# Forget-gate attention pairs: k's hi and lo parts by thirds, and the last v product in eight steps among maxima and key blocks

## The chip, the core and the metric

One core of a Trainium2 chip runs the whole program. The metric is the device time of one execution, in microseconds (us). Engines in the rows: PE is TensorE (PEld its weight loads), DVE is VectorE, ACT is ScalarE, POOL is GpSimd, SP is SyncE, which issues the DMAs. Each engine works through its own queue in order; semaphores tie them together.

## The reference

One step of a hybrid encoder layer over 1024 prompt rows and 32 sample rows of width 1024: a SwiGLU block, a mixer, a second SwiGLU block, all in float32. The change lies in one of the mixer's three head groups, the forgetting attention (8 heads of 64, here in 4 pairs of heads):

```python
q, k, v, f_logit = ...                      # columns of rms(x) @ w_in
q = rms_per_head(q) * gq;  k = rms_per_head(k) * gk
logf = log_sigmoid(f_logit + b_f)
k_all, v_all = concat(past_k, k), concat(past_v, v)
cum = cumsum(concat(past_logf, logf))
s = q @ k_all.T * 64 ** -0.5 + cum_q[:, None] - cum_k[None, :]
s = where(kpos <= qpos, s, -inf)
y = softmax(s) @ v_all                      # k, v and logf are outputs too
```

The matrix products keep float32 precision: each operand is split into a hi part (rounded to fp32r) and a lo part (the rest), and a product is hi*hi + hi*lo + lo*hi.

## The kernel before

`MIXER` runs two conv groups, four "fox" groups (one pair of forget-gate heads each, `attend(g)` for g = 0 to 3, called first to fourth pair here) and two memory groups. The pairs begin at about 919, 1014, 1101 and 1188 us; the memory groups follow at 1274. Engines run separate programs, and `attend(g)` exists once for each.

**Projections.** `PROJ["fox"]` lists nine products, n = 0 to 8: q, k and v, each in three chunks of rows (384, 384, 288 columns of the moving operand, `CHUNKS`). `product` works through the 8 blocks of the model width (KT), three matmuls to a block (L252 to L254), into the bank `PBANK[n]`. For q and k, ScalarE squares the result (L1201), TensorE sums the squares over a head (`head_sums`, L1999), ScalarE makes a rough 1/root with Ln and Exp (`head_rough`, L875 and L877, banks 6 and 7 in turn), VectorE refines it and scales (`normed`: L1294, L1296, L1298, L1658) into `qT` or `kT`. For v, ScalarE copies to `vT` (L1196). `bank_free` lets a product into a used bank only when its reader is done: product 6 (the first of v) takes bank 0, which held q's first chunk and then the turned cached keys (`turn_past`, copied by `past_keys`, L1124).

**Parts of k.** ScalarE writes q's hi parts (`q_hi(c)`, L1138 and the like, after products 2, 3 and 4) and, after product 7, both hi parts of k over all 1184 keys (`k_hi`, L1130). VectorE copies the other halves (`k_twice`, L1666) and makes the lo parts (`k_lo`, L1673), after all three k chunks.

**Tokens.** `TT` lists the turns of k and v to token-major layout (`turn_tokens`, L2037; ScalarE copies them out in `tokens`, L1147 for k, L1150 for v): three for k, three for v. SyncE stores them (`store_tokens`). In the first pair TensorE also turns the forget sums (L2152) once `tokens(0)` is copied, and only then SyncE loads the minus-F rows (L637).

**Maxima.** `scores(n)`, L2062, for 18 units (2 of samples, 8 row tiles for each head) in banks 6-7 and 4-5 by turns; VectorE takes each row's maximum (`smax`, L1694). `scores(1)` waits until the k tokens are out of banks 4 and 5; from n = 2, `scores(n)` waits for `smax(n-2)`, from n = 10 for `smax(n-1)`. `turn_max` and `turn_four` (L2076, L2077) turn the maxima to rows, ScalarE copies them (`maxima`, L1164). Units 10 to 17 lie in the next stretch.

**Key blocks.** For each of 28 blocks: `keyed(n)` (scores with keys on the partitions, L2104, L2105, mask L2107), `exps(n)` on ScalarE (L1175), and two blocks later `weigh(n-2)` (L2120). `keyed(0)` waits for the first two rows of maxima.

GpSimd splits the next group's weights (`split_in`, L804 and L787) when this group's products and k parts are done.

Of the kernel before, what the change touches and what calls it, by code (L numbers as in the profile page):

```python
# [31 lines left out]
def hybrid_step(nc, i, o):  # L32
# [30 lines left out]
    with ctx:  # L63
# [198 lines left out]
        PBANK = {"fox": [0, 1, 2, 3, 4, 5, 0, 1, 2], "mem": [0, 1, 2, 3, 4]}  # L262
# [16 lines left out]
        def nrm_count(kind, m):  # L279
# [4 lines left out]
        TT = {"fox": [("k", 0, 4, 3), ("k", 4, 4, 4), ("k", 8, 1, 5), ("v", 0, 4, 0), ("v", 4, 4, 1), ("v", 8, 1, 3)],  # L284
              "mem": [("k", 0, 2, 3), ("v", 0, 2, 4)]}
# [21 lines left out]
        KEND = {"fox": KEYS, "mem": 2 * NMEM}  # L307
# [42 lines left out]
        NB = {k: len(BLOCKS[k]) for k in BLOCKS}  # L350
        NSTORED = {"fox": 96, "mem": 48}
# [89 lines left out]
        def _(sp):  # L441
# [198 lines left out]
            def store_tokens(g):  # L640
# [4 lines left out]
                last = NTT["fox"] // 2 if kind == "fox" else 1  # L645
# [92 lines left out]
        def _(pool):  # L738
# [56 lines left out]
            def split_in(v):  # L795

                if MIXER[v - 1][0] == "conv":
                    pool.wait_ge(CONVS["proj"], 9 * v)
                else:
                    pool.wait_ge(A["proj"], upto(NPROJ, v - ITER["conv"]))  # L800
                    pool.wait_ge(A["kdve"], 4 * (v - ITER["conv"]))
# [52 lines left out]
        def _(act):  # L854
# [255 lines left out]
            def attend(g):  # L1110
# [9 lines left out]
                def past_keys():  # L1120
                    act.wait_ge(A["cturned"], g + 1)
                    act.wait_ge(A["kdve"], 4 * g)
# [3 lines left out]
                def k_hi():  # L1126
                    act.wait_ge(A["past"], g + 1)
                    act.wait_ge(A["nrm"], nrm0 + NRM[kind])
                    for j in range(PAIR):
                        act.activation(KS1[half_rows(j), j, 0:KEND[kind]], kT[half_rows(j), 0:KEND[kind]], ACT.Copy)\  # L1130
                            .then_inc(A["khi"], 1)
# [9 lines left out]
                def tokens(q):  # L1141
                    what, t0, nt, b = TT[kind][q]
                    act.wait_ge(A["tturned"], tt0 + q + 1)
                    n = tile_rows(kind, t0)
                    src = bank(b, nt * P, n).rearrange("p (t n) -> p t n", t=nt)
# [43 lines left out]

                if g == 0:  # L1190
                    act.wait_ge(s_init, 7)
                for n, (what, _, c) in enumerate(PROJ[kind]):
                    s, w = span(kind, n)
                    act.wait_ge(A["proj"], proj0 + n + 1)
                    if what == "v":
                        act.activation(vT[:, s:s + w], bank(PBANK[kind][n], w), ACT.Copy).then_inc(A["vcopied"], 1)  # L1196
                    else:
                        m = NORMED[kind].index(n)
# [14 lines left out]
                    if n in (2, 3, 4):  # L1213
                        q_hi(n - 2)
                    if kind == "fox" and n == 7:
                        k_hi()
                        act.wait_ge(A["stored"], upto(NSTORED, g))
                        tokens(0)
                    if kind == "fox" and n == 8:
                        tokens(1)  # L1220
                        tokens(2)
                if kind == "mem":
                    k_hi()
# [3 lines left out]
                else:  # L1227
                    tokens(3)
                    tokens(4)
                    tokens(5)  # L1230
# [52 lines left out]
        def _(dve):  # L1283
# [357 lines left out]
            def attend(g):  # L1641
# [19 lines left out]
                def k_twice():  # L1661

                    dve.wait_ge(A["past"], g + 1)
                    dve.wait_ge(A["nrm"], nrm0 + NRM[kind])
                    for j in range(PAIR):
                        dve.tensor_copy(KS1[half_rows(1 - j), j, 0:KEND[kind]], kT[half_rows(j), 0:KEND[kind]])\  # L1666
                           .then_inc(A["kdve"], 1)

                def k_lo():
                    for j in range(PAIR):  # L1670
                        dve.wait_ge(A["khi"], 2 * g + j + 1)
                        r = half_rows(j)
                        dve.tensor_tensor(KS2[r, j, 0:KEND[kind]], kT[r, 0:KEND[kind]],  # L1673
                                          KS1[r, j, 0:KEND[kind]].bitcast(F32), ALU.subtract).then_inc(A["kdve"], 1)

# [41 lines left out]
                for m in range(NSQ[kind]):  # L1717
# [68 lines left out]
        def _(pe):  # L1786
# [28 lines left out]
            def product(b, block, x_hi, x_lo, s, w, fresh=None):  # L1815


                for k in range(KT):
# [166 lines left out]
            def attend(g):  # L1985
# [36 lines left out]
                def turn_tokens(q):  # L2022
                    what, t0, nt, b = TT[kind][q]
# [231 lines left out]
```

## Time and profile before

| | |
|---|---|
| median of 3 runs | 2303.93 us (2303.18 to 2308.80) |
| profiled execution, its time | 2305.36 us |
| profiled execution, its span | 2303.2 us |
| mean granted TensorE clock | 0.955 |
| busy in the span | PE 92%, PEld 87%, DVE 52%, ACT 36%, POOL 15% |
| first to last instruction of TensorE's second pair | 1014.5 to 1100.7 us |

A row of a timeline reads: start, duration, engine, line, operation, output<-inputs, shapes, how many instructions were merged (x2), and in brackets how long the engine stood before it and who ended that wait. A duration of x2 is from the first's start to the last's end. A granted clock of 1.00 is 2.4 GHz, 0.50 is 1.2 GHz.

### The profile page before, as it was taken

The numbers are of one execution on the slowest core, as the hardware profiler recorded it, in microseconds if no ns is written. First come the engines' busy times: TensorE is split into PE (matmuls) and PEld (weight loads), VectorE is DVE, ScalarE is ACT, GpSimd is POOL, SyncE is SP. The second block draws the span as 40 slices with busy tenths as digits, with TensorE's granted clock in tenths as the row PEclk, the third lists the DMA queues.
The fourth block names the chain that finished last, engine by engine and source line by source line (L and its number), as shares of the span: only waits on it lengthen the run. The fifth ranks groups of instructions, "written<-read, shape, count | busy, mean of one in ns | idle before, by whom it ended". The sixth has DMA issues, their size and how long they took to land.

```text
span 2303.2 us, 37130 instructions
## 1 busy us (share of the span) xinstructions
PE 2115.3 (92%) x15188; PEld 1994.7 (87%) x15188; DVE 1206.0 (52%) x2097; ACT 824.8 (36%) x1375; POOL 346.7 (15%) x175
## 2 busy tenths in 40 slices
PE   4889999999999879799999779968899999999996
PEld 3789999999999879676876657958899999999996
DVE  6795665586330072545545555179755666843103
ACT  5342223244231240455555454054322223533213
POOL 0000000003444423101101203000000000143440
PEclk7899999999999989899999889979999999999997
DMA  4542222247543216321220125024322223485222
GB/s 150 140 121 75 84 84 70 78 131 290 176 130 92 93 57 47 90 61 42 57 61 22 47 84 184 1 94 147 91 76 77 84 84 99 152 297 168 89 68 85
DMA packets 239736, 234.76 MB, mean 102 GB/s; under 512 B 28297, under 2 KB 181513, under 8 KB 239057
## 3 DMA queue, kind: packets, MB, share of 16 engines
q1 hardware_dynamic: 239568, 232.39, 33.6%
q8 instruction: 122, 2.00, 0.4%
q14 instruction: 46, 0.37, 0.1%
HBM read 182.56 MB, written 49.80 MB: 101 GB/s over the span
## 4 chain that ended last, share of the span: by engine, by line
PE 81%; DVE 10%; issue 3%; ACT 3%; DMA 2%; SPq 1%; POOL 0%; DVEq 0%; ACTq 0%
PE banks L252 23%; PE banks L253 23%; PE banks L254 23%; PE banks L2120 4%; PE banks L2062 1%; PE banks L2104 1%; PE banks L1833 1%; PE banks L2105 1%; DVE scores_minusF L1694 1%; DVE hforms_lo L1459 1%; DVE w_lo L1353 1%; DMA x_again<-x_spill 1%; DMA out_conv_state_sample<-conv_in 1%; PE banks L1999 1%; DVE hforms_f L1443 1%
## 5 line engine op out<-in xcount | busy, mean ns | idle before, releaser
L252 PE MATMUL banks<-hforms_hi,w_hi 128*128 128x264 f32 x2112 | 607.2, 288 | 57.0 <-issue 34.0
L253 PE MATMUL banks<-hforms_lo,w_hi 128*128 128x264 f32 x2112 | 607.7, 288 | 0.0
L254 PE MATMUL banks<-hforms_hi,w_lo 128*128 128x264 f32 x2112 | 606.1, 287 | 0.0
L252 PEld LDWEIGHTS banks<-hforms_hi,w_hi 128*128 128x128 f32 x2112 | 404.6, 192 | 61.9 <-issue 47.7
L780 POOL TENSOR_TENSOR w_lo<-w_raw,w_hi 128x1024 fp32r<-128x1024 f32 x88 | 219.3, 2496 | 1382.3 <-ACT w_hi L985 1382.3
L254 PEld LDWEIGHTS banks<-hforms_hi,w_lo 128*128 128x128 f32 x2112 | 403.6, 191 | 0.0
L253 PEld LDWEIGHTS banks<-hforms_lo,w_hi 128*128 128x128 f32 x2112 | 403.2, 191 | 0.0
L254 PE MATMUL banks<-acts_a,w_lo 128*128 128x264 f32 x896 | 256.5, 286 | 0.0
L252 PE MATMUL banks<-acts_a,w_hi 128*128 128x264 f32 x896 | 254.4, 284 | 1.7 <-DVE acts_a L1477 1.7
L253 PE MATMUL banks<-acts_a,w_hi 128*128 128x264 f32 x896 | 255.2, 285 | 0.0
L252 PE MATMUL banks<-h_hi,w_hi 128*128 128x384 f32 (+1 forms) x576 | 198.0, 344 | 23.0 <-DVE h_lo L1311 10.2
L985 ACT ACTIVATE w_hi<-w_raw 128x1024 fp32r<-128x1024 f32 x88 | 93.2, 1059 | 348.3 <-PE banks L254 307.0
L253 PE MATMUL banks<-h_lo,w_hi 128*128 128x384 f32 (+1 forms) x576 | 189.1, 328 | 0.0
L254 PE MATMUL banks<-h_hi,w_lo 128*128 128x384 f32 (+1 forms) x576 | 188.1, 327 | 0.0
L1493 DVE SCALAR_TENSOR_TENSOR xT<-banks,xT 128x264 f32<-128x264 f32 x64 | 23.9, 432 | 298.0 <-PE banks L254 298.0
L252 PEld LDWEIGHTS banks<-acts_a,w_hi 128*128 128x128 f32 x896 | 170.1, 190 | 2.2 <-issue 2.0
L254 PEld LDWEIGHTS banks<-acts_a,w_lo 128*128 128x128 f32 x896 | 168.4, 188 | 0.0
L253 PEld LDWEIGHTS banks<-acts_a,w_hi 128*128 128x128 f32 x896 | 168.3, 188 | 0.0
L918 ACT ACTIVATE w_hi<-w_sums 128x1024 fp32r<-128x1024 f32 x90 | 95.6, 1062 | 190.1 <-DVE w_sums L1341 116.1
L254 PE MATMUL banks<-acts_b,w_lo 128*128 128x264 f32 x512 | 146.6, 286 | 0.0
L253 PE MATMUL banks<-acts_b,w_hi 128*128 128x264 f32 x512 | 145.8, 285 | 0.0
L252 PE MATMUL banks<-acts_b,w_hi 128*128 128x264 f32 x512 | 145.2, 284 | 0.0
(257 smaller groups left out, 4101.9 us busy)
## 6 DMA issues: line engine op xcount, KB each, us to landing
w_raw<-in_w_ffn_down SPq DMA_DIRECT2D x88, 512.0 KB, 4.2
w_raw<-in_w_ffn_gate SPq DMA_DIRECT2D x60, 512.0 KB, 5.2
w_raw<-in_w_ffn_up SPq DMA_DIRECT2D x60, 512.0 KB, 5.2
act_rows<-act_f SPq DMA_DIRECT2D x44, 528.0 KB, 2.8
acts_f<-act_rows SPq DMA_DIRECT2D x44, 528.0 KB, 5.2
xT<-x_spill SPq DMA_DIRECT2D x3, 4224.0 KB, 16.6
w_raw<-in_w_in SPq DMA_DIRECT2D x20, 512.0 KB, 6.0
x_spill<-xT SPq DMA_DIRECT2D x4, 2112.0 KB, 9.3
```

Source lines behind the costliest of these rows:

```text
L252: eng.matmul(out, w_hi, x_hi, start=first, stop=False, skip_group_check=added)
L253: eng.matmul(out, w_hi, x_lo, start=False, stop=False, skip_group_check=added)
L254: return eng.matmul(out, w_lo, x_hi, start=False, stop=last, skip_group_check=added)
L780: pool.tensor_tensor(wlo[:, e % 4, :], raw[:, e % 4, :], whi[:, e % 4, :].bitcast(F32), ALU.subtract)\
L918: act.activation(slots(whi, wxh, G[q], n), src, ACT.Copy).then_inc(f[f"{which}_hi"], 1)
L985: act.activation(whi[:, e % 4, :], raw[:, e % 4, :], ACT.Copy).then_inc(f["wd_hi"], 1)
L1353: dve.tensor_tensor(slots(wlo, wxl, slot, 1), r[:, at:at + 1, :], slots(whi, wxh, slot, 1).bitcast(F32), ALU.subtract).then_inc(f[f"{which ...
L1443: dve.scalar_tensor_tensor(q[:, first:last + 1:last - first, :], x.rearrange("p (h n) -> p h n", h=2), gain[:, 2 * n, k:k + 1], nr[:, s:s ...
L1459: dve.tensor_tensor(HL[z][:, :, kk, :], FT[:, m % 2, 0:7, :], HH[z][:, :, kk, :].bitcast(F32), ALU.subtract).then_inc(f["forms_lo"], 1)
L1493: dve.scalar_tensor_tensor(xT[:, d, s:s + QC], bank(DBANK[e], QC), 0.5, xT[:, d, s:s + QC], ALU.mult, ALU.add).then_inc(f["resid"], 1)
L1694: dve.tensor_tensor_reduce(junk[0:rows, 0:w], PS[0:rows, b:b + w], nF[0:rows, j, k0:k0 + w], 1.0, -3e38, ALU.add, ALU.max, m).then_inc(A[" ...
L2120: pe.matmul(PS[:, 512 * ob + oc:512 * ob + oc + w], VO[0:kr, vo, j, :], PRT[0:kr, (b0 + n) % 4, 0:w], start=first, stop=last, skip_group_c ...
```

## The change

- k's parts are made in thirds (`KPARTS`), each as soon as its chunk is scaled. ScalarE does `k_hi(0)`, `k_hi(1)`, `k_hi(2)` at the end of steps n = 4, 5, 6 of its projection loop, VectorE `k_parts(c)` right behind `normed(3 + c)`. The last third (with the cached keys, 416 columns) also waits for `past_keys`. q's last third moves from n = 4 to n = 3 on ScalarE, and its lo part from m = 3 to m = 2 on VectorE.
- Product 8 (the last of v) leaves the projections. TensorE does its blocks 0 to 2 between `scores(9)` and `turn_four(0, 1)`, behind a wait for `smax(8)` (it now uses bank 7), blocks 3 and 4 behind `turn_four(0, 1)`, and blocks 5, 6 and 7 in the key-block steps 0, 1 and 2.
- The v tokens become four turns: tiles 0 to 3, 4 and 5 in the maxima as before, tiles 6 and 7 and tile 8 (bank 7) at step 5 of the key blocks. ScalarE's v copy of product 8 stands behind `exps(2)`, its copies of the two turns behind `exps(5)`.
- Waits follow: `scores(0)` for all hi parts and copies, GpSimd for all nine products, `weigh` of v tiles 6 to 8 for the last copy, SyncE's v stores likewise. The memory groups compute as before.

```diff
-        PBANK = {"fox": [0, 1, 2, 3, 4, 5, 0, 1, 2], "mem": [0, 1, 2, 3, 4]}
+        PBANK = {"fox": [0, 1, 2, 3, 4, 5, 0, 1, 7], "mem": [0, 1, 2, 3, 4]}
+        V_EARLY, V_TURNED = 3, 5
+        V_BEHIND = {-1: (3, 4), 0: (5,), 1: (6,), 2: (7,)}
+        KPARTS = {"fox": [(0, 384), (384, 384), (768, KEYS - 768)], "mem": [(0, 2 * NMEM)]}
...
 # ScalarE
-                def k_hi():
-                    act.wait_ge(A["past"], g + 1)
-                    act.wait_ge(A["nrm"], nrm0 + NRM[kind])
+                def k_hi(c):
+                    s, w = KPARTS[kind][c]
+                    if c == NKP[kind] - 1:
+                        act.wait_ge(A["past"], g + 1)
+                    act.wait_ge(A["nrm"], nrm0 + nrm_count(kind, 3 + c))
...
-                    if n in (2, 3, 4):
-                        q_hi(n - 2)
+                    for c in {"fox": {2: (0,), 3: (1, 2)}, "mem": {2: (0,), 3: (1,), 4: (2,)}}[kind].get(n, ()):
+                        q_hi(c)
+                    if kind == "fox" and n in (4, 5, 6):
+                        k_hi(n - 4)
...
                     exps(n)
+                    if kind == "fox" and n == max(V_BEHIND):
+                        v_copy(8)
+                    if kind == "fox" and n == V_TURNED:
+                        tokens(5)
+                        tokens(6)
...
 # VectorE
-                    if m == 3:
+                    if m == (2 if kind == "fox" else 3):
                         q_lo(2)
-                k_twice()
-                k_lo()
+                    if m >= 3:
+                        k_parts(m - 3)
...
 # TensorE
+                def last_v(steps):
+
+                    s, w = span(kind, 8)
+                    for k in steps:
+                        if k == 0:
+                            pe.wait_ge(A["smax"], 18 * g + 9)
+                        mm = product(PBANK[kind][8], 2, hh, hl, s, w, None, (k,))
+                        if k == KT - 1:
+                            mm.then_inc(A["proj"], 1)
...
                 scores(9)
+                if kind == "fox":
+                    last_v(range(V_EARLY))
                 turn_four(0, 1)
+                if kind == "fox":
+                    last_v(V_BEHIND[-1])
                 for n in range(NB[kind] + 2):
                     if n < NB[kind]:
                         keyed(n)
                     if n >= 2:
                         weigh(n - 2)
+                    if kind == "fox":
+                        last_v(V_BEHIND.get(n, ()))
+                        if n == V_TURNED:
+                            turn_tokens(5)
+                            turn_tokens(6)
```

## Rows read from the trace of the kernel before

**Rows 1.** The page, chain that ended last, shares of the span by engine.
```profile
PE 81%; DVE 10%; issue 3%; ACT 3%; DMA 2%; SPq 1%; POOL 0%; DVEq 0%; ACTq 0%
```

**Rows 2.** Timeline of ScalarE, third pair, 1118 to 1141 us.
```profile
1122.85 0.49 ACT L1201 ACTIVATE head_squares<-banks 128x384 f32<-128x384 f32 x1 [1.12 <-PE banks L254]
...
1124.70 0.90 ACT L1138 ACTIVATE q_hi_lo<-qT 64x288 fp32r<-64x288 f32 x2
...
1126.78 0.41 ACT L1201 ACTIVATE head_squares<-banks 128x288 f32<-128x288 f32 x1 [0.25 <-PE banks L254]
...
1131.59 0.49 ACT L1196 ACTIVATE vT<-banks 128x384 f32<-128x384 f32 x1 [3.02 <-PE banks L254]
...
1136.65 2.40 ACT L1130 ACTIVATE k_hi_twice<-kT 64x1184 fp32r<-64x1184 f32 x2
...
1139.07 0.60 ACT L1147 ACTIVATE k_by_token<-banks 128x512 f32<-128x512 f32 x1
...
1140.32 0.74 ACT L1147 ACTIVATE k_by_token<-banks 128x512 f32<-128x512 f32 x2
```

**Rows 3.** Timeline of VectorE, third pair, refinement of k's thirds to maximum 0.
```profile
1124.67 0.56 DVE L1294 SCALAR_TENSOR_TENSOR head_rstd<-banks,head_r 128x384 f32<-128x384 f32 x1 [1.79 <-ACT head_r L877]
...
1126.45 0.62 DVE L1658 SCALAR_TENSOR_TENSOR kT<-banks,head_gains,head_rstd 128x384 f32<-128x384 f32 x1
...
1133.09 0.46 DVE L1294 SCALAR_TENSOR_TENSOR head_rstd<-banks,head_r 128x288 f32<-128x288 f32 x1 [2.08 <-ACT head_r L877]
...
1134.57 0.64 DVE L1658 SCALAR_TENSOR_TENSOR kT<-banks,head_gains,head_rstd 128x256 f32<-128x256 f32 x2
...
1137.86 2.80 DVE L1673 TENSOR_TENSOR k_lo_and_one<-kT,k_hi_twice 64x1184 fp32r<-64x1184 f32 x2 [0.98 <-ACT k_hi_twice L1130]
...
1140.71 0.31 DVE L1694 CUSTOM_DVE_ANT_0 scores_minusF<-banks,minusF 32x160 f32<-32x160 f32 x1
```

**Rows 4.** Timeline of TensorE, third pair: first k tokens, scores 1, `keyed(0)`.
```profile
1136.07 0.60 PE L2037 MATMUL banks<-ident,kT 128*128 128x128 f32 x4
...
1141.11 0.26 PE L2062 MATMUL banks<-k_hi_twice,q_hi_lo 128*32 128x160 f32 x1 [0.54 <-ACT k_by_token L1147]
...
1150.45 0.80 PE L2104 MATMUL banks<-q_hi_lo,k_hi_twice 128*128 128x512 f32 x1 [0.68 <-ACT q_hi_and_max L1164]
```

**Rows 5.** Windows: length, PE, PEld, DVE, ACT, POOL busy, clock, DMA share, GB/s.
```profile
960.00:985.00 25.00, 18.60 (x90) 12.17 (x88) 9.26 (x33) 6.40 (x17) 10.08 (x6) 0.73 0.58 157
...
1053.00:1073.00 20.00, 16.57 (x86) 10.82 (x85) 10.77 (x31) 7.62 (x20) 10.07 (x6) 0.91 0.22 55
...
1139.00:1159.00 20.00, 16.79 (x82) 10.69 (x80) 10.40 (x30) 7.67 (x20) 10.09 (x6) 0.83 0.22 54
...
1158.00:1178.00 20.00, 18.98 (x92) 11.77 (x91) 8.95 (x16) 11.40 (x21) 0.00 (x0) 1.00 0.20 65
...
1149.00:1150.00 1.00, 0.33 (x1) 0.13 (x1) 0.40 (x2) 0.19 (x1) 1.00 (x1) 0.93 0.00 0
...
1150.00:1151.00 1.00, 0.55 (x1) 0.50 (x2) 0.00 (x0) 0.40 (x1) 1.00 (x1) 0.50 0.02 8
```

**Rows 6.** Timeline of TensorE, third pair, last matmuls of two blocks of product 8.
```profile
1139.15 0.30 PE L254 MATMUL banks<-h_hi,w_lo 128*128 128x288 f32 x1
...
1139.55 0.30 PE L254 MATMUL banks<-h_hi,w_lo 128*128 128x288 f32 x1
```

**Rows 7.** Timelines of ScalarE, TensorE, SyncE, VectorE and TensorE, first pair.
```profile
945.31 0.91 ACT L1138 ACTIVATE q_hi_lo<-qT 64x288 fp32r<-64x288 f32 x2 [0.75 <-DVE qT L1658]
...
946.34 0.81 PE L1999 MATMUL banks<-head_squares,ones_over_head 128*128 128x384 f32 x2
...
960.83 0.82 SPq L637 DMA_DIRECT2D minusF<-negF_rows  x2
...
966.82 0.31 DVE L1694 CUSTOM_DVE_ANT_0 scores_minusF<-banks,minusF 32x160 f32<-32x160 f32 x1 [4.88 <-DMA minusF<-negF_rows]
...
978.29 0.50 PE L2104 MATMUL banks<-q_hi_lo,k_hi_twice 128*128 128x512 f32 x1 [0.68 <-ACT q_hi_and_max L1164]
```

More of the change, by code:

```diff
@@ L350, in hybrid_step @@
         NB = {k: len(BLOCKS[k]) for k in BLOCKS}
+        NKP = {k: len(KPARTS[k]) for k in KPARTS}
         NSTORED = {"fox": 96, "mem": 48}
@@ L644, in store_tokens @@
                 c = it * P
-                last = NTT["fox"] // 2 if kind == "fox" else 1
+                last = 3 if kind == "fox" else 1
                 sp.wait_ge(A["tcopied"], upto(NTT, g) + last)
@@ L1141, in tokens @@
                 def tokens(q):
-                    what, t0, nt, b = TT[kind][q]
-                    act.wait_ge(A["tturned"], tt0 + q + 1)
+                    what, t0, nt, b, at = TT[kind][q]
+                    act.wait_ge(A["tturned"], tt0 + max(x for x, y in enumerate(TT[kind]) if y[0] == what and y[3] == b) + 1)
                     n = tile_rows(kind, t0)
-                    src = bank(b, nt * P, n).rearrange("p (t n) -> p t n", t=nt)
+                    src = PS[0:n, 512 * b + at:512 * b + at + nt * P].rearrange("p (t n) -> p t n", t=nt)
                     if what == "k":
@@ L1188, in sum_rough, with v_copy @@
                     act.activation(lr[r, 0:w], lr[r, 0:w], ACT.Exp, scale=-1.0).then_inc(A["rough_sum"], 1)
+                def v_copy(n):
+                    s, w = span(kind, n)
+                    act.wait_ge(A["proj"], proj0 + n + 1)
+                    act.activation(vT[:, s:s + w], bank(PBANK[kind][n], w), ACT.Copy).then_inc(A["vcopied"], 1)
                 if g == 0:
@@ L1193, in attend @@
                     s, w = span(kind, n)
-                    act.wait_ge(A["proj"], proj0 + n + 1)
+                    if kind == "fox" and n == 8:
+                        break
                     if what == "v":
-                        act.activation(vT[:, s:s + w], bank(PBANK[kind][n], w), ACT.Copy).then_inc(A["vcopied"], 1)
+                        v_copy(n)
                     else:
+                        act.wait_ge(A["proj"], proj0 + n + 1)
                         m = NORMED[kind].index(n)
@@ L1227, in attend @@
                 else:
-                    tokens(3)
-                    tokens(4)
-                    tokens(5)
+                    for q in range(1, 5):
+                        tokens(q)
                 for x in range(3):
@@ L1813, in norm_mean, with product @@
                 pe.matmul(bank(MBANK + c, w), onesD[:, :], nsum[:, 0:w], start=True, stop=True).then_inc(NORM[n]["mean"], 1)
-            def product(b, block, x_hi, x_lo, s, w, fresh=None):
-                for k in range(KT):
+            def product(b, block, x_hi, x_lo, s, w, fresh=None, steps=range(KT)):
+                for k in steps:
                     if fresh:
@@ L2022, in turn_tokens @@
                 def turn_tokens(q):
-                    what, t0, nt, b = TT[kind][q]
+                    what, t0, nt, b, at = TT[kind][q]
                     if kind == "mem":
@@ L2083, in turn_four @@
                             pe.wait_ge(A["mcopied"], 5 * g + 4)
+                        else:
+                            pe.wait_ge(A["tcopied"], tt0 + NTT[kind])
                     elif h:
-                        pe.wait_ge(A["tcopied"], tt0 + NTT[kind])
+                        pe.wait_ge(A["tcopied"], tt0 + 1)
+                        if g == 0:
+                            pe.wait_ge(fg["copied"], 5)
                     else:
@@ L2108, in keyed, with e_of @@
                     mm.then_inc(A["keyed"], 1)
+                def e_of(vo):
+                    return 6 <= vo <= PT
+                def last_v(steps):
+                    s, w = span(kind, 8)
+                    for k in steps:
+                        if k == 0:
[3 more added lines that the diff above has]
+                            mm.then_inc(A["proj"], 1)
                 def weigh(n):
@@ L2114, in weigh @@
                     if n == 0:
-                        pe.wait_ge(A["tcopied"], tt0 + NTT[kind])
+                        pe.wait_ge(A["tcopied"], tt0 + (5 if kind == "fox" else 2))
+                    elif kind == "fox" and e_of(vo):
+                        pe.wait_ge(A["tcopied"], tt0 + 7)
                     if q0 == SEQ and first:
@@ L2124, in attend @@
                     s, w = span(kind, n)
+                    if kind == "fox" and n == 8:
+                        break
                     pe.wait_ge(W["lo"], 3 * v + b + 1)
```

56 lines of the change are left out of this document (24 added, 32 removed).

## The prediction

> **What bounds the kernel now.** I read the page first: TensorE carries four fifths of the chain that ended last [rows 1]. The change touches only the four forget-gate pairs, which run between 919 and 1274 us. There I read the timeline of each engine for the third pair (the second and fourth repeat it to about 0.4 us), looking for places where TensorE stands, and then the windows for the clock.
>
> A pair has three stretches. In the projections TensorE is never kept waiting from the second pair on. ScalarE and VectorE run behind it: square, sum on TensorE, rough root on ScalarE (L875, L877), VectorE's refinement and scaling (L1294 to L1658) [rows 2, 3]. Then come the maxima. Scores 0 starts when the last product is done, scores 1 when ScalarE has copied k's turned tokens [rows 2, 4]. From there VectorE sets the pace, until the second group of four maxima is turned and copied; TensorE idles before `keyed(0)` at 1150.45 [rows 4]. Last come the key blocks, where TensorE is full, 18.98 of 20 us [rows 5].
>
> The clock matters as well. In the microsecond from 1149 TensorE is busy for 0.33 us, and at its end the granted clock goes from 1.0 to 0.5, that is from 2.4 to 1.2 GHz [rows 5]. From the mean clocks, half speed lasts 2*(1-0.91)*20 = 3.6 us in the second pair, 2*(1-0.83)*20 = 6.8 us in the third and 2*(1-0.73)*25 = 13.5 us in the first, whose gap while the minus-F rows are loaded is long [rows 5, 7].
>
> **The maxima do not start when the last product leaves.** The last v product, 288 columns, is eight blocks with 0.40 us from one to the next [rows 6], 3.2 us. Taking it out of the projections would start the maxima 3.2 us earlier if k's parts were ready. They aren't, because of ScalarE's new order. `k_hi(c)` stands in ScalarE's queue ahead of the next square or v copy, which stand ahead of the next rough root, and VectorE's next refinement needs that root. What was two engines overlapping becomes one chain. Per third:
> - VectorE's refinement, 1124.67 to 1126.45+0.62: 2.40; for the last, narrower third 1133.09 to 1134.57+0.64: 2.12 [rows 3].
> - `k_hi(c)`: two instructions. 288 columns take 0.90/2 = 0.45, 1184 take 2.40/2 = 1.20 [rows 2]; in between, 384 columns are about 0.53 and 416 about 0.56. A third is 1.07, the last 1.12.
> - square or v copy, then rough root: v copy at 1131.59 to refinement at 1133.09, 1.50 [rows 2, 3].
>
> The third thirds of q come ahead of the k parts too: a pair of q instructions of 0.9, twice, 1.8 us, go into an idle gap of 1.12 [rows 2], and delay the next square by 0.7 and the root behind it by 0.5. Sum for the third pair: 1124.67+0.5 = 1125.2; +2.40 +1.07 +1.50 = 1130.1; +2.40 +1.07 +1.50 = 1135.1; +2.12 = 1137.2. Before it was 1134.57+0.64 = 1135.2, so k is finished 2.0 us **later**. Then ScalarE: 1.12 for its last part, 0.4 for the v copy that waits behind it, 0.60+0.74 for the k tokens: 1140.1. It was 1140.32+0.74 = 1141.06 [rows 2]. Scores 1, which started at 1141.11, gains **1.0 us**, not 3.2. VectorE's own share (it copies the other halves while ScalarE works, and two differences of a third take 2.8*416/1184, about 1.0, against 2.80) ends near 1139.3, and the whole-width copy and difference no longer hold scores 0; they aren't last [rows 3]. TensorE stands from 1136.1 (first k tokens, [rows 4]) to 1137.2, turns nine tiles in about a microsecond and stands again to 1140.1.
>
> **The maxima and their gap.** Three of the nine v turns leave (four take 0.60, so about 0.1 each in a row); they end a short wait of VectorE: 0.1 to 0.2 more. The first three blocks start when maximum 8 is done and take 1.2 us, in TensorE's idle time, but the turns of maxima 6 to 8 now queue behind them: up to 0.1 lost. Blocks 3 and 4, 0.8 us, lie beside ScalarE's copy of the row of maxima (idle 0.68 [rows 4]); 0.1 sticks out. `keyed(0)`: 1.1 us earlier.
>
> **The key blocks.** Three blocks, 1.2 us, stand on full TensorE, and three turns, 0.3 to 0.45. Each change from scores or values to a product costs a first matmul that starts its successor late: none to 0.15 each way here, estimated, since no row shows these neighbours. Sum 1.5 to 2.2; I take **1.9**, near the top, since TensorE has no slack there. ScalarE's v copy and token copies are added behind exps 2 and 5; they wait for TensorE, and exps 3 and 6 wait behind them. Values are consumed two blocks later, so I cost this at nothing; without that lag it would be the copies, 0.4 and about 1. GpSimd's split of the next weights now waits for the last block, some 13 us later; it takes 10.09 us, GpSimd is idle for the next 20 [rows 5], and the next pair starts at 1188: nothing. SyncE's v stores wait for tokens 6, some 13 us later, ahead of the minus-F load, which waits for the last maximum anyway: nothing.
>
> Per pair without the clock: -1.1+1.9 = +0.8.
>
> **The clock.** Five blocks in the gap before `keyed(0)` keep TensorE busy there, and the late fall should go. While TensorE is full, half speed costs half its length: (3.6+6.8+3.6)/2 = 7.0 in the second to fourth pair (the fourth falls like the second), less 0.5 for what TensorE stands in it [rows 5]. Gain 6.5. But a **new gap** opens, 1136.1 to 1140.1, four microseconds with about one of work. The old fall came in a gap with a third of work [rows 5], so I expect a fall here in two or three of the four. It hits the maxima, where VectorE sets the pace: in the first pair, at half speed, maximum 0 to `keyed(0)` was 978.29-966.82 = 11.5 us, in the third 1150.45-1140.71 = 9.7 [rows 3, 4, 7]. Price 1.5 each, to 1.8.
>
> The Trainium skill, "TensorE: Matmul & The Clock Gate", section "HAM oscillation — how this bites in real kernels", says that a product whose work between two waits is short is throttled in every round and starts cold each time. By that rule the time would be -0.8+4.5, 2307.6, since all three pairs would pay; the trace agrees so far that every pair has its fall.
>
> **The first pair** is worse off. ScalarE waits for q's last third, which VectorE's forget sums delay: it starts at 945.31 [rows 7] and takes 1.8. Square 0.5, root 1.1 and past keys 0.25 behind it end at 948.95. The head sum of k's first third waits for that square instead of running at 946.34, and the first v product, about 0.4 behind it (half of 0.81 for two), waits for the past keys' bank [rows 7]: TensorE stands 2.2 us. The chain gives 948.7 +2*(2.40+1.07+1.50) +2.12 = 960.8 for k. The turn of the F rows waits for the first k tokens' copy (1.12+0.4+0.6 later, 962.9), the load of minus F is issued 0.8 behind, 963.7 instead of 960.83, and maximum 0 hangs on that load (a wait of 4.88 [rows 7]). **+2.9**, +1.9 in the key blocks, -1.5 if a second fall near 979 goes: +3.3.
>
> **Sum.** 3*0.8 - 6.5 + 3.3 = -0.8; with new falls in two to three pairs, 3 to 4.5 more: +2 to +4. I take +2.1. The profiled execution's span of 2303.2 becomes 2305.3, its time 2305.4 becomes 2307.5; the median lay 1.4 lower, 2303.93, and becomes **2306.0**.
>
> **Rivals.**
> - *The order of ScalarE does not bind* (the change's obvious promise). Maxima start 3.1 us earlier in every pair, the first one's load 2.8: 4*(1.9)-3*3.1-2.8-6.5-1.5 = -12.5, 2291.4. For it: TensorE alone. Against: k's root stands behind `k_hi` in one queue, and ScalarE is in order.
> - *The new gap does not lower the clock.* Nine turns may be work enough: -0.8 and some stalls less than reckoned, 2300 to 2303.
> - *Slower: half speed outlasts the maxima.* In the first pair it lasted through the whole of the maxima. If the fall in the new gap still holds at `keyed(0)`, the old 6.5 is not gained and the early five blocks take twice as long, +1.0 a pair: 3*(0.8+1.5+1.0), and 2.9+1.9+1.0 in the first, = +15.7 less what a part of the pairs escapes; 10 to 16, 2314 to 2320. It decides when half speed lasts over 10 us from 1138.
>
> **How the numbers follow.** Forecast with two or three new falls 0.50 (2302 to 2311), clock kept 0.24, half speed through the gap 0.15, order not binding 0.11. A measurement tells about 0.3% from none, 6.9 us. Of the forecast nearly all is within that; a tenth of the rival with the clock kept is beyond it, and most of the third. Faster 0.12, same 0.74, slower 0.14. Stages behind the pairs run unchanged, but their own clock falls may shift by a microsecond or two. Range for 8 in 10: 2297 to 2314, which leaves out the ends of both far rivals; the likeliest case's own is 2302 to 2311.
>
> **What would show it.** Right: ScalarE's k parts each directly followed by a square or v copy that was ready long before; the last refinement of k near 2 us later in the pair; TensorE with one microsecond of work in four before scores 1; the last product's blocks 0 to 4 at full clock in the old gap; in the first pair 2 us of standing ahead of the first v product, minus F issued 3 us later. Wrong: maxima 3 us earlier, or key blocks no longer than before (then the steps fell into waits I don't see), or clock falls at places that follow no gap.

## The result, and the profile after

The changed kernel took 2314.27 us in the median of five runs (2309.83 to 2315.76), the kernel before 2305.01 in the median of five beside it (2303.18 to 2308.80): ratio 1.0037, interval 1.0022 to 1.0052. Later, on another chip, it was 2311.35 (12 runs) against 2306.27 (26 runs): 1.0023, interval 1.0012 to 1.0035. So the change costs between 0.1 and 0.5%, about what was taken for the limit of what can be told. The forecast was 2306.0 within 2297 to 2314. The first median lies 0.3 us above that range, the second within it. One execution of the late `k_hi` below (8570.1 us) and one of the move only (2352.76) were in a slow state, and no ratio here uses them.

The profiled execution took 2309.83, its span was 2307.7 against 2303.2. The page, the second row as in [rows 1]:

```profile
PE 2121.9 (92%) x15188; PEld 1999.7 (87%) x15188; DVE 1211.2 (52%) x2129; ACT 828.8 (36%) x1399; POOL 347.0 (15%) x175
...
PE 80%; DVE 9%; ACT 4%; issue 3%; DMA 2%; SPq 1%; POOL 0%; DVEq 0%; ACTq 0%
```

These shares say nothing on the change. It is seen pair by pair. Lengths in us, each worked out from the first product of a pair to that of the next (the first pair from the turn of the past keys on); "memory" are the two groups behind the pairs, which run the same steps in both kernels:

| | 1st | 2nd | 3rd | 4th | pairs | memory |
|---|---|---|---|---|---|---|
| before | 71.46 | 86.21 | 87.26 | 85.93 | 330.9 | 130.9 |
| changed | 74.75 | 87.82 | 87.23 | 86.81 | 336.6 | 135.1 |

The pairs lost 5.7 us, the memory groups 4.2; the stretch ahead of the pairs was 4.6 shorter, the one behind the memory groups 0.9 shorter: +4.5 with rounding, the difference of the spans. The repeats below tell which of these belong to the change.

The second pair of the changed kernel, which answers to [rows 2] and [rows 3]. First ScalarE, then VectorE. For comparison with the third pair of before, subtract 1035.76 here and 1123.30 there, the turns of the past keys.

```profile
1034.22 0.91 ACT L1147 ACTIVATE q_hi_lo<-qT 64x288 fp32r<-64x288 f32 x2
1036.10 0.49 ACT L1217 ACTIVATE head_squares<-banks 128x384 f32<-128x384 f32 x1
...
1040.21 1.07 ACT L1139 ACTIVATE k_hi_twice<-kT 64x384 fp32r<-64x384 f32 x2 [2.30 <-DVE kT L1676]
1041.31 0.41 ACT L1217 ACTIVATE head_squares<-banks 128x288 f32<-128x288 f32 x1
...
1045.35 1.08 ACT L1139 ACTIVATE k_hi_twice<-kT 64x384 fp32r<-64x384 f32 x2 [2.46 <-DVE kT L1676]
1046.45 0.49 ACT L1202 ACTIVATE vT<-banks 128x384 f32<-128x384 f32 x1
...
1050.20 1.12 ACT L1139 ACTIVATE k_hi_twice<-kT 64x416 fp32r<-64x416 f32 x2 [2.25 <-DVE kT L1676]
...
1051.74 1.21 ACT L1156 ACTIVATE k_by_token<-banks 128x512 f32<-128x512 f32 x3
```

```profile
1037.79 0.56 DVE L1312 SCALAR_TENSOR_TENSOR head_rstd<-banks,head_r 128x384 f32<-128x384 f32 x1 [1.47 <-ACT head_r L884]
...
1042.92 0.56 DVE L1312 SCALAR_TENSOR_TENSOR head_rstd<-banks,head_r 128x384 f32<-128x384 f32 x1 [0.80 <-ACT head_r L884]
...
1047.98 0.46 DVE L1312 SCALAR_TENSOR_TENSOR head_rstd<-banks,head_r 128x288 f32<-128x288 f32 x1 [0.72 <-ACT head_r L884]
...
1049.46 0.64 DVE L1676 SCALAR_TENSOR_TENSOR kT<-banks,head_gains,head_rstd 128x256 f32<-128x256 f32 x2
```

Each engine waits for the other in turn: ScalarE's `k_hi(c)` for VectorE's scaled third, VectorE's next refinement for ScalarE's root, with a square or v copy right behind each `k_hi` that had long been ready. The refinements stand 5.13 and 5.06 apart. VectorE stands 0.80 and 0.72 us before the second and the third of them, for ScalarE's root: its own parts of k, which now lie between the refinements too, don't hold them.

TensorE in the same pair, answering to [rows 4]:

```profile
1050.16 1.20 PE L2052 MATMUL banks<-ident,kT 128*128 128x128 f32 x9 [1.48 <-DVE kT L1676]
1051.58 0.23 PE L2076 MATMUL banks<-k_hi_twice,q_hi_lo 128*32 128x160 f32 x1 [0.21 <-ACT k_hi_twice L1139]
...
1053.00 0.34 PE L2076 MATMUL banks<-k_hi_twice,q_hi_lo 128*32 128x160 f32 x1 [1.07 <-ACT k_by_token L1156]
...
1064.91 0.50 PE L2122 MATMUL banks<-q_hi_lo,k_hi_twice 128*128 128x512 f32 x1
```

It waits 1.48 for k, turns nine tiles, and waits twice more. The windows (length, busy time of PE, PEld, DVE, ACT, POOL, clock, DMA share, GB/s) are the new gap and the maxima of the second pair, twenty microseconds of the second, third and fourth, and the second pair's key blocks:

```profile
1050.00:1053.00 3.00, 1.55 (x11) 1.12 (x12) 2.34 (x7) 2.70 (x6) 0.00 (x0) 0.90 0.00 0
...
1053.00:1063.00 10.00, 9.88 (x39) 7.05 (x40) 6.02 (x17) 2.07 (x7) 0.00 (x0) 0.52 0.19 55
...
1050.00:1070.00 20.00, 18.43 (x92) 13.76 (x93) 10.09 (x31) 7.70 (x19) 0.92 (x1) 0.74 0.10 28
...
1138.00:1158.00 20.00, 18.10 (x96) 13.41 (x96) 9.98 (x30) 8.20 (x19) 1.61 (x2) 0.83 0.10 28
...
1228.00:1248.00 20.00, 19.70 (x100) 14.13 (x101) 9.27 (x28) 6.61 (x15) 4.72 (x4) 0.83 0.10 28
...
1068.00:1088.00 20.00, 18.97 (x91) 11.63 (x90) 7.46 (x15) 11.17 (x24) 10.12 (x6) 1.00 0.32 91
```

After the gap the maxima run at 0.52, half speed. By the means it lasts 2*(1-0.74)*20 = 10.4 us in the second pair and 6.8 in the third and fourth. TensorE looks busier there than before (9.88 of 10) and yet does the maxima more slowly. The fall is in the maxima of all three pairs, and the late one of [rows 5] is gone.

### The profile page after: what moved, and what is told of

Its sections match the earlier page's. It is cut to its first block, busy times and chain, and to the rows that moved or that the text cites. A ratio compares the mean times of both kernels' runs of the same rounds, so it can differ in the third digit from the quotient of the medians.

```text
span 2307.7 us, 37198 instructions
## 1 busy us (share of the span) xinstructions
PE 2121.9 (92%) x15188; PEld 1999.7 (87%) x15188; DVE 1211.2 (52%) x2129; ACT 828.8 (36%) x1399; POOL 347.0 (15%) x175
## 4 chain that ended last, share of the span: by engine, by line
PE 80%; DVE 9%; ACT 4%; issue 3%; DMA 2%; SPq 1%; POOL 0%; DVEq 0%; ACTq 0%
PE banks L252 23%; PE banks L253 23%; PE banks L254 22%; PE banks L2154 4%; PE banks L2076 2%; PE banks L1851 1%; PE banks L2122 1%; PE banks L2123 1%; DMA x_again<-x_spill 1%; DVE hforms_lo L1477 1%; DMA out_conv_state_sample<-conv_in 1%; DVE w_lo L1371 1%; DVE scores_minusF L1712 0%; DVE head_rstd L1316 0%; DVE head_rstd L1314 0%
```

## The experiments

Between what the maxima wait for (k's order), the clock in the new gap, and the product's blocks in the key blocks, the times alone can't decide, since they overlap. So each part was done alone, undone alone, or covered. Times in the following table are us from the turn of the past keys, second, third and fourth pair (one figure where all agree):

| | scores 1 | maximum 0 | `keyed(0)` |
|---|---|---|---|
| before | 17.81 | 17.41 | 27.54, 27.15, 27.15 |
| changed | 17.24 | 16.48 | 29.15, 28.56, 28.15 |
| thirds only | 19.50 | 19.10 | 28.83, 28.84, 29.18 |
| move only | 17.04 | 17.40 | 28.42, 28.77, 28.36 |
| late `k_hi` | 15.12 | 15.95 | 25.27, 26.82, 26.64 |
| gap filled | 17.24 | 16.48 | 26.75, 26.74, 27.11 |
| product in the maxima | 15.12 | 15.96 | 25.08, 25.28, 25.43 |
| q's last third back | 16.79 | 16.04 | 28.04, 27.70, 26.65 |

**The changed kernel again.** No edit.

> The changed kernel once more, unchanged, beside the others. Theory A (ScalarE's queue makes one chain of k's thirds, the new gap of four microseconds lowers the clock, and what is left of the difference is clock falls in the memory groups that differ from execution to execution): the four pairs are again longer by 3.3, 1.6, 0.0 and 0.9 us within 1 us each, since their instructions repeat; the memory groups and the stretch ahead of the pairs may differ by 2 to 5 us from the first profile; median +5 to +10. Theory B (the memory groups are slower by the change itself): they are again 4 us longer than in the kernel before.

2311.35 us, ratio 1.0023. The profiled execution was its longest, span 2315.4: pairs 75.10, 87.22, 86.78, 86.66, together 335.8; memory groups 136.7. The pairs repeat, with a fall in each again. In the fourth it was short this time, 2*(1-0.91)*20 = 3.6 us:

```profile
1228.00:1248.00 20.00, 17.55 (x100) 12.88 (x100) 10.41 (x31) 8.24 (x20) 2.30 (x2) 0.91 0.10 28
```

**Thirds only**: k's parts by thirds in the kernel before, with q's last third one step earlier as in the change; the last product stays where it was.

```diff
-                    if n in (2, 3, 4):
-                        q_hi(n - 2)
+                    for c in {"fox": {2: (0,), 3: (1, 2)}, ...}[kind].get(n, ()):
+                        q_hi(c)
-                        k_hi()
+                    if kind == "fox" and n in (4, 5, 6):
+                        k_hi(n - 4)
...
-                k_twice()
-                k_lo()
+                    if m >= 3:
+                        k_parts(m - 3)
```

> The kernel before with k's parts by thirds alone, product 8 where it was. Theory A: k is finished 2.0 us later, TensorE stands 1.4 us before the first k tokens with product 8 still behind them, scores 1 starts 1.4 us later, the late clock fall before keyed(0) stays: +1.4 a pair, +4 to +5 in the first, +9 in all. Rival (the thirds are free or a gain, and the moved product costs): within 1 us of before in each pair, or faster, since the last difference on VectorE is a third as long.

2316.63 us (6 runs), ratio 1.0045, 1.0029 to 1.0061. TensorE, second pair (the turn of the past keys at 1041.25), and the window of its maxima and key blocks:

```profile
1055.63 0.66 PE L2041 MATMUL banks<-ident,kT 128*128 128x128 f32 x4 [1.45 <-DVE kT L1662]
...
1060.73 0.26 PE L2066 MATMUL banks<-k_hi_twice,q_hi_lo 128*32 128x160 f32 x1 [0.54 <-ACT k_by_token L1150]
...
1060.00:1104.00 44.00, 39.90 (x199) 24.56 (x197) 18.64 (x49) 23.43 (x52) 9.61 (x6) 1.00 0.19 55
```

The first k tokens come 14.38 after the turn, against 12.77 before (1136.07-1123.30): the new order costs 1.6 us ahead of the tokens in each pair, 1.7 at scores 1. About 0.44 of it is q's last third (the run with that third back, below), the other 1.2 k's thirds. The last product then fills what was the new gap, and the clock stays up: second pair 86.13, no longer than before. The fourth is 86.47, the third 87.70 with a fall behind `keyed(0)`. The expectation had the late fall in every pair; it is missing in the second and the fourth, and why isn't settled. The first pair is hit hardest: 78.47, +7.0. The four together take 338.8, 7.7 more than before. This is the part of the change that costs.

**The move only**: the changed kernel with k's parts whole again, and they and q's last third where they were.

```diff
-        KPARTS = {"fox": [(0, 384), (384, 384), (768, KEYS - 768)], ...}
+        KPARTS = {"fox": [(0, KEYS)], ...}
...
                     if kind == "fox" and n == 7:
+                        k_hi(0)
...
+                k_parts(0)
```

> The changed kernel with k whole again (hi parts, copies and lo parts after the last third, q's last third where it was), so the moved product alone. Theory A: the gap on TensorE is there too, since k's whole parts and tokens take ScalarE until 4 us after product 7; scores 1 gains 0.6 us, VectorE's whole difference holds maximum 0, key blocks +1.9, clock falls in the new gap instead of the old one: +0.6 a pair, first pair 0, +2 in all. Rival (the moved product is the loss): +1.5 a pair or more, like the changed kernel.

2309.42 us (12 runs), ratio 1.0018, 1.0005 to 1.0031. Second pair, VectorE's difference and what TensorE waits for; then its window:

```profile
1050.14 2.81 DVE L1690 TENSOR_TENSOR k_lo_and_one<-kT,k_hi_twice 64x1184 fp32r<-64x1184 f32 x2 [0.97 <-ACT k_hi_twice L1139]
...
1051.58 0.24 PE L2074 MATMUL banks<-k_hi_twice,q_hi_lo 128*32 128x160 f32 x1 [2.08 <-DVE k_lo_and_one L1690]
...
1052.62 0.26 PE L2074 MATMUL banks<-k_hi_twice,q_hi_lo 128*32 128x160 f32 x1 [0.70 <-ACT k_by_token L1156]
...
1048.00:1068.00 20.00, 16.66 (x91) 12.63 (x90) 11.41 (x28) 8.37 (x17) 0.00 (x0) 0.83 0.10 28
```

Scores 1 is 0.77 earlier than before, but maximum 0 stays at 17.40: VectorE starts it behind its 2.81 of whole-width difference. The gap is there and with it the fall; `keyed(0)` comes 0.9 to 1.6 us later than before. The first pair takes 71.20, as before. The four together take 332.8, +1.8. Thirds or move, each alone is slower than before; together, at 2311.35, they lie between the two.

**`k_hi` one place later, q's last third back**: the changed kernel, with ScalarE's k thirds behind the square or v copy and root that VectorE needs next, VectorE's parts one step later as well, and q's last third as in the kernel before (by the same lines as under "Q's last third back" below).

```diff
-                    if kind == "fox" and n in (4, 5, 6):
-                        k_hi(n - 4)
+                    if kind == "fox" and n in (5, 6):
+                        k_hi(n - 5)
+                    if kind == "fox" and n == 6:
+                        k_hi(2)
...
-                    if m >= 3:
-                        k_parts(m - 3)
+                    if kind == "fox" and m >= 4:
+                        k_parts(m - 4)
+                if kind == "fox":
+                    k_parts(2)
```

> The changed kernel with ScalarE's k_hi(0) and k_hi(1) one step later, behind the next rough root, k_hi(2) behind k_hi(1), q's last third where it was, and VectorE's parts one step later likewise. Theory A: ScalarE no longer waits for VectorE ahead of a root, k is finished when it was in the kernel before, scores 1 starts 2.8 us earlier than before, TensorE's gap before it is about 2 us and no clock fall follows: -3 a pair, -2.5 in the first, -12 us in all, faster than both. Rival (ScalarE's order does not matter, the moved product costs): like the changed kernel, +5 to +9.

2298.76 us, ratio 0.9966, 0.9955 to 0.9977: faster than before. ScalarE and TensorE in the second pair (turn at 1032.67), then the windows of the second and third:

```profile
1044.70 1.12 ACT L1139 ACTIVATE k_hi_twice<-kT 64x416 fp32r<-64x416 f32 x2 [1.28 <-DVE kT L1678]
...
1045.44 1.14 PE L2058 MATMUL banks<-ident,kT 128*128 128x128 f32 x9
...
1047.50 0.24 PE L2082 MATMUL banks<-k_hi_twice,q_hi_lo 128*32 128x160 f32 x1 [0.92 <-DVE k_hi_twice L1688]
1047.78 0.27 PE L2082 MATMUL banks<-k_hi_twice,q_hi_lo 128*32 128x160 f32 x1
```

```profile
1045.00:1065.00 20.00, 17.54 (x105) 12.68 (x104) 12.14 (x35) 8.37 (x20) 2.82 (x2) 1.00 0.10 28
...
1129.00:1149.00 20.00, 18.64 (x98) 13.31 (x96) 11.48 (x33) 7.81 (x19) 1.31 (x2) 0.83 0.10 28
```

The k tokens come at 12.77 again, without a wait (1045.44-1032.67), and scores 1 at 15.12, 2.7 us earlier than before. That is nearly the gain that the first rival promised, and what withheld it was the order of the queues. This run moves both ScalarE's and VectorE's; that ScalarE's was the one that bound is read from the waits of the changed kernel above. Maximum 0 gains less, 1.5 us (15.95 against 17.41): VectorE starts it behind its own parts of k. The pairs are 69.52, 83.96, 85.49, 85.33, together 324.3 against 330.9. The expectation had -12 us with no clock fall; it was -7.5. The third and fourth still fall to half speed, the second doesn't, though the three have the same instructions at the same times up to maximum 0. Why the second escapes is not settled.

**The gap filled**: the changed kernel with 17 matmuls of 288 columns in the gap of each pair, nine ahead of the k tokens and eight between scores 0 and scores 1. Their result is used by nobody; all else is computed as before.

```diff
                     if kind == "fox" and n == 7:
+                        filler(9)
                         turn_tokens(0)
...
                 scores(0)
+                if kind == "fox":
+                    filler(8)
                 scores(1)
```

> The changed kernel with 17 matmuls of 288 columns added in the new gap of each pair, whose result nobody reads: 9 (1.2 us) ahead of the first k tokens, 8 (1.0 us) between scores 0 and scores 1. Both are places where TensorE stands 1.5 and 1.1 us. Theory A (the new gap lowers the clock, and half speed over the maxima costs 2.3 to 3.3 us): no fall behind the gap in pairs two to four, maximum 0 to keyed(0) about 9.5 us instead of 11.5 to 12.7, each pair 2 to 3 us shorter, 6 to 8 in all. Rival (more matmuls are more work, or the fall comes from the maxima themselves): pairs as long as before this edit or longer by 0.5.

2309.30 us (10 runs) against 2309.97 on the same chip (17 runs): 1.0008, 0.9995 to 1.0020. TensorE's k tokens, second pair, and the windows that answer to those of the changed kernel:

```profile
1054.13 1.20 PE L2052 MATMUL banks<-ident,kT 128*128 128x128 f32 x9 [0.28 <-DVE kT L1676]
...
1053.00:1073.00 20.00, 18.42 (x115) 13.70 (x113) 11.46 (x34) 8.22 (x20) 2.25 (x2) 1.00 0.10 28
...
1139.00:1159.00 20.00, 18.27 (x112) 13.39 (x111) 11.19 (x34) 8.62 (x20) 2.82 (x2) 1.00 0.10 28
...
1224.00:1244.00 20.00, 18.06 (x113) 13.35 (x112) 11.11 (x34) 8.14 (x19) 2.04 (x2) 1.00 0.10 28
```

In these three pairs scores 1 and maximum 0 start where they did in the changed kernel, so up to there nothing else moved; the clock stays at 1.0 and `keyed(0)` comes 2.4, 1.8 and 1.0 earlier. The fourth is 0.4 later than its twins (27.11) without any fall, after VectorE stood once for 0.49 us in the maxima. The first pair keeps its long gap at the load of minus F and its fall. The pairs are 85.44, 85.42, 85.79, the first 74.54: together 331.2, where the three executions of the changed kernel have 336.6, 335.8 and 335.5. That the idle gap lowers the clock, and what this costs, is shown by this run.

**The product in the gap and in the maxima**: the order of the late `k_hi`, product 8 in steps of its blocks where TensorE stood (two ahead of the scores, one at maximum 6, one at 8, four behind the ninth scores), none left in the key blocks; maximum 0 writes to bank 0, so that bank 2 is free for the product.

```diff
-        V_BEHIND = {-1: (3, 4), 0: (5,), 1: (6,), 2: (7,)}
+        V_AT = {0: (0, 1), 6: (2,), 8: (3,), 9: (4, 5, 6, 7)}
...
-        PBANK = {"fox": [0, 1, 2, 3, 4, 5, 0, 1, 7], ...}
+        PBANK = {"fox": [0, 1, 2, 3, 4, 5, 0, 1, 2], ...}
```

> The kernel with the late k_hi (e3_late_k_hi), and product 8 in bank 2: blocks 0 and 1 ahead of scores 0, 2 behind scores 6, 3 behind scores 8, 4 to 7 behind scores 9, its v copy ahead of the copy of the second four maxima, the turns of v tiles 6 to 8 right behind that turn; the first maxima are turned into bank 0. No block lies in the key blocks any more. Theory A: the key-block stretch falls from 36.1 to 34.8 us, keyed(0) moves by no more than 0.3, the clock falls in fewer pairs: pairs of 82.5 to 83.5, 5 to 8 us less than e3_late_k_hi, 13 to 15 less than the kernel before. Rival (the blocks are on the path wherever they stand): pairs as in e3_late_k_hi, 84 to 85.5.

2293.0 us (6 runs), ratio 0.9940, 0.9922 to 0.9957: it beats both kernels. Windows over the maxima and the key blocks of the second pair, and over the maxima of the third and fourth:

```profile
1046.00:1066.00 20.00, 19.20 (x112) 13.24 (x110) 12.39 (x36) 8.63 (x23) 8.76 (x6) 1.00 0.10 28
...
1058.00:1078.00 20.00, 18.88 (x90) 11.31 (x90) 8.20 (x19) 10.62 (x23) 9.14 (x6) 1.00 0.32 92
...
1130.00:1150.00 20.00, 19.09 (x105) 12.48 (x104) 11.88 (x35) 7.84 (x22) 10.13 (x6) 1.00 0.11 31
1212.00:1232.00 20.00, 18.84 (x107) 12.67 (x107) 11.77 (x35) 7.82 (x22) 9.50 (x6) 1.00 0.10 28
```

No fall in these pairs. They take 67.97, 82.36, 82.56, 82.71, together 315.6, 15.3 less than before. From `keyed(0)` to the next pair it is 34.72 us, where the changed kernel has 36.11 at full clock too: three blocks and three turns in the key blocks cost 1.39. The thirds only agree: 34.73 in the two pairs without a fall. GpSimd's split of the next weights lies in the key blocks here too (9.14 of 20 us) and costs nothing there, as forecast. The expectation of 82.5 to 83.5 a pair held but for 0.1.

**Q's last third back**: the changed kernel with `q_hi(2)` one step later on ScalarE and `q_lo(2)` one later on VectorE.

```diff
-                    for c in {"fox": {2: (0,), 3: (1, 2)}, ...}[kind].get(n, ()):
-                        q_hi(c)
+                    if n in (2, 3, 4):
+                        q_hi(n - 2)
...
-                    if m == (2 if kind == "fox" else 3):
+                    if m == 3:
                         q_lo(2)
```

> The changed kernel with q's last third alone where it was (ScalarE step 4, VectorE behind m = 3). Theory A: in the first pair TensorE no longer stands before k's head sum; it still waits for the past keys' bank only if ScalarE is late, so 1.5 to 2.2 us come back there; in the others k is finished up to 0.5 us earlier, the pairs change by less than 0.7. Rival: the first pair's loss is the chain of k's thirds and the load of minus F alone, no change there.

2307.93 us, one run. Scores 1 comes 0.44 earlier than in the changed kernel (16.79 against 17.23), which prices the move of q's last third in the later pairs. In the first pair the head sum of k's first third (L2017) runs without the wait that it has in the changed kernel, shown in the section below:

```profile
945.50 0.81 PE L2017 MATMUL banks<-head_squares,ones_over_head 128*128 128x384 f32 x2
```

The first pair is 72.46 against 74.75: 2.3 of the 3.3 that it lost come from q's last third, not from k's.

The other three take 86.72, 86.36 and 85.34. The second and third are 0.4 to 0.5 shorter than where the changed kernel has a fall of the same length (87.22, 86.78). The fourth is 1.3 shorter, more than the 0.7 expected, since its clock does not fall:

```profile
1137.00:1157.00 20.00, 17.70 (x94) 13.12 (x94) 10.78 (x33) 7.89 (x19) 1.10 (x2) 0.83 0.10 28
1224.00:1244.00 20.00, 16.87 (x101) 12.18 (x102) 10.88 (x34) 8.61 (x20) 2.79 (x2) 1.00 0.10 28
```

The four together are 330.9, what the kernel before takes. So in this one execution the whole loss of the change is gone once q's last third stands where it was; about 1 us of that is the fall that the fourth pair was spared.

**The kernels again**, no edit: before, before, changed.

> The kernel before, unchanged, for a second profile. Theory A: the four pairs repeat to within 1 us (71.5, 86.2, 87.3, 85.9), with one late clock fall each; the memory groups, 130.9 us in the first profile, may be 133 to 137 here, as in every profile of the changed kernels, because their clock falls differ by execution. Theory B (the change slows the memory groups): 131 again.

> The kernel before a third time, to settle the memory groups, whose two profiles so far gave 130.9 and 131.1 us against 132.3 to 136.8 in every kernel with an edit. If clock falls that fit differently to each execution are the cause: anything from 131 to 137, with the falls at other places relative to the group's start. If the edit slows them: 131 a third time.

> The changed kernel a third time, for the same question: memory groups 131 to 137 by the clock, 135 to 137 again if the edit slows them. The pairs again +3.3, and +0 to +1.6 each.

Times 2304.75, 2310.91, 2314.61. Pairs together 331.2, 331.0, 335.5; memory groups 131.1, 135.6, 136.5. In the third execution of before the long late fall is in the second pair (87.82) and the short one in the third (86.00), the other way round than in the first two. Here the windows over the memory groups, the first execution of before, the changed kernel, and the third execution of before:

```profile
1274.00:1405.00 131.00, 100.57 (x455) 73.67 (x453) 67.90 (x141) 67.14 (x137) 24.08 (x12) 0.82 0.25 76
```

```profile
1274.00:1410.00 136.00, 106.32 (x457) 76.84 (x456) 68.65 (x141) 67.56 (x138) 24.08 (x12) 0.78 0.24 74
```

```profile
1274.00:1409.00 135.00, 106.11 (x453) 77.36 (x451) 67.29 (x138) 66.97 (x136) 24.09 (x12) 0.76 0.24 74
```

The kernel before has the long memory groups too, at as low a clock. So the 4.2 us there are not a cost of the change alone: with the same instructions the kernel before shows 130.9, 131.1 and 135.6. Whether the changed kernel (135.1, 136.7, 136.5) draws the long form more often isn't settled. All nine profiled executions of kernels with an edit have it, 134.6 to 136.8. But the times show no fixed cost outside the pairs: medians against before, less the difference of the pairs, give +0.2 for the changed kernel on the second chip, +2.6, +1.4, -0.8, -0.8 and -1.5 for thirds only, move only, late `k_hi`, gap filled and product in the maxima. What belongs to the change is in the pairs: a mean of 336.0 against 331.0, **+4.9 us**, with each of the three above each of the other three.

## Why the prediction was right, and where its sizes were off

The direction and the mechanism held: the change turns a stall late in the maxima into one ahead of them, and gives nothing. The size did not: +2.1 us was forecast, the pairs alone lost 4.9. By its steps:

- **k is finished later, not earlier.** Forecast 2.0 us; it was 14.34 after the turn (1049.46+0.64-1035.76) against 11.91, 2.4. The first refinement is at 2.03 against 1.37 (forecast +0.5, was +0.7), and the steps of 5.13 and 5.06 were forecast as 4.97. Thirds alone and the late `k_hi` show it from both sides: 12.77 for the k tokens before, 14.4 with the thirds, 12.77 again with them late. Of the 1.6 at the tokens q's last third is 0.44.
- **Scores 1** gained 0.57, forecast 1.0. The missing 0.4 is the 0.4 that k came later.
- **`keyed(0)` without the clock**: 26.75 with the gap filled, against 27.15 to 27.54, a gain of 0.4 to 0.8 in the second and third pair and none in the fourth (27.11), where 1.1 was forecast. 0.4 of the shortfall is the later k again; the rest isn't traced.
- **Key blocks**: 1.39 a pair, forecast 1.9 within 1.5 to 2.2. Three blocks of 0.40 alone are 1.2; the turns and changes of kind cost almost nothing. I had taken a value near the top, and it lay just under the range.
- **The late fall** is gone from all three pairs, as forecast. From `keyed(0)` to the next pair it was 36.11, 37.54 and 36.21 before. Without fall and blocks it is 34.72. So the falls cost 1.39, 2.82 and 1.49, together 5.7; forecast 6.5.
- **The new fall** was forecast for two or three pairs at 1.5. It came in all three, in each of the three executions. Against the filled gap, maximum 0 to `keyed(0)` is 12.66, 12.09 and 11.65 instead of 10.27, 10.27 and 10.62: 2.4, 1.8 and 1.0. In the execution that followed it was 1.8, 1.4 and 0.9.
- **The first pair**: +3.3 forecast, +3.3 measured, but not by the same terms, so that the agreement is luck. TensorE stood for 1.7 us (forecast 2.2), and maximum 0 came 3.85 later (27.61 against 23.76), forecast 2.9:

```profile
943.11 0.91 PE L2017 MATMUL banks<-head_squares,ones_over_head 128*128 128x384 f32 x2 [1.21 <-ACT head_squares L1217]
944.52 0.41 PE L252 MATMUL banks<-h_hi,w_hi 128*128 128x384 f32 x1 [0.51 <-ACT kT L1131]
...
960.01 0.82 SPq L644 DMA_DIRECT2D minusF<-negF_rows  x2
966.06 0.31 DVE L1712 CUSTOM_DVE_ANT_0 scores_minusF<-banks,minusF 32x160 f32<-32x160 f32 x1 [4.54 <-DMA minusF<-negF_rows]
```

  The load is issued 21.56 after the turn of the past keys (960.01-938.45) against 17.77. `keyed(0)` is 3.4 later, and the key blocks gave back 0.1 where +0.4 was forecast: the second fall was worth its 1.5, the blocks 1.39.

**The sum.** Pairs 2 to 4 by the measured sizes: `keyed(0)` is 4.0 later in all (85.86 against 81.84), of it -1.2 without the clock (the filled gap has 80.60) and +5.3 from the new falls. Behind it 4.2-5.7 = -1.5. Together +2.5, where the forecast had -1.1 to +0.4. The first pair adds 3.3: +5.7 in the first execution, +4.9 over three. The terms that were off are the count and price of the new falls (5.3 against 3 to 4.5), `keyed(0)` without the clock (-1.2 against -3.3), and the late falls (5.7 against 6.5); the overestimate of the key blocks, 1.5 in all, hid about a third of it. The forecast also took +2.1 where its own terms with two to three falls give +2.2 to +3.7. The rest of the 9.3 us between the first medians isn't explained by the pairs: the clock in the memory groups is one part that the traces show, and in the later comparison the difference is 5.1.

**The rivals.** *The order of ScalarE does not bind*, 2291.4: false for the change, but nearly right on what lay behind that order. With the late `k_hi` scores 1 came 2.7 earlier in pairs 2 to 4 (it had 3.1), maximum 0 only 1.5, and `keyed(0)` 2.3 in the one pair without a fall. *The new gap does not lower the clock*, 2300 to 2303: false. With the clock kept by filler the pairs were at 331.2, as before, not 1 to 4 under it; it would have needed the scores' full gain as well. *Half speed outlasts the maxima*: its condition, over 10 us, was met in the second pair (10.2 us, from 1052.4 to 1062.6), but the clock was back before `keyed(0)` at 1064.91, since half speed itself had pushed that later. Its premise that half speed lasted through the whole of the first pair's maxima was a misreading of the mean: the 13.5 us are two falls, 10.2 us from 965.6 on and 3.4 behind `keyed(0)` (978.29), with full clock between them:

```profile
976.00:977.00 1.00, 0.24 (x2) 0.04 (x1) 1.00 (x1) 0.00 (x0) 1.00 (x2) 1.00 0.00 0
977.00:978.00 1.00, 0.32 (x1) 0.13 (x1) 0.23 (x2) 0.35 (x1) 0.92 (x2) 1.00 0.00 0
```

The rule of the Trainium skill ("TensorE: Matmul & The Clock Gate", section "HAM oscillation — how this bites in real kernels") had every pair pay, which would have put the forecast at 2307.6. That section of the Trainium skill has it of work that is shorter than the wait beside it. For the changed kernel the traces agree: about 1.5 us of work among 2.8 us of waits (1.48, 0.21 and 1.07 in the second pair), and nine falls in nine pairs. The variants don't follow so simply. The late `k_hi` shows a second pair that doesn't fall with the gap shortened to one wait of 0.92, while its twins do.

## What to carry over

Before work is put earlier on an in-order engine, ask what stands behind it in that queue and who waits for that: one `k_hi` ahead of each root cost 1.2 us a pair here and q's last third another 0.4, and one place later both were free. A step taken out of a full stretch to shorten it can leave a gap, and here the gap lowered TensorE's clock for the stretch behind. Put the moved work into the idle places, not into the next full stretch, which pays for all of it. Compare stretches, not only totals: here the four pairs together repeat to about a microsecond while the whole moves by ten or more.

## What the runs showed of the hardware

- A fall of TensorE's clock costs even where VectorE sets the pace: 0.9 us (3.6 us at half speed) to 2.4 (10.4 us) in the maxima, against 1.4 for 3.6 us and 2.8 for 6.8 where TensorE is full.
- 17 matmuls of 288 columns whose result nobody uses, in a gap that other engines set, bought about 5 us over four pairs (336.0 to 331.2, the latter in one execution). Idle TensorE is not free here.
- The same instructions at the same distances needn't fall alike: the second pair of the late `k_hi` kept its clock, the third and fourth did not; the memory groups of one kernel took 130.9 and 135.6 us. The runs of the kernel before spread from 2302.5 to 2312.4 on one chip and from 2298.3 to 2311.8 on another. A fall in one execution is no proof of a cause; one that comes in nine pairs of nine and goes with filler in three of three is.
